# Low parts of weights and the S5 parameters moved from VectorE to GpSimd in a one-core model kernel

## The chip, the core and the metric

The kernel runs on one core of a Trainium2 chip. The metric is device time in microseconds (us), median of three runs. The engines are TensorE (PE in the rows, PEld for its weight loads), VectorE (DVE), ScalarE (ACT), GpSimd (POOL) and SyncE (SP), which issues the DMAs of the weight stream. They run side by side and meet at semaphores.

## The reference, cut to what matters

Two model blocks follow each other on 256 tokens of width 2048: four mixers (SSD, FOX attention, MLA attention, S5), each with a residual and a layer norm, then a mix of attention heads, a cross attention and a feed-forward part. All matmuls are float32. The part that is changed most is the S5 mixer:

```python
u, z = jnp.split(h @ w_in, 2, axis=-1)
lam = lax.complex(lam_re, lam_im)
step = jnp.exp(log_step)[:, None]
lam_bar = jnp.exp(lam * step)
b_bar = ((lam_bar - 1.0) / lam)[..., None] * lax.complex(b_re, b_im)
bu = jnp.einsum('gpi,btgi->btgp', b_bar, ug)
_, states = lax.associative_scan(_diag_linear_combine, (a_seq, bu), axis=1)
y = jnp.einsum('gip,btgp->btgi', c, states).real.reshape(bsz, T, S5_WIDTH) + d_skip * u
y = jax.nn.gelu(y)
y = y * jax.nn.sigmoid(y @ w_glu + b_glu)
y = y * jax.nn.silu(z)
```

## The kernel before, in words

**Weight slots.** All weights come as one stream of 575 slots of 128 x 2048 float32 (1 MB; some slots are narrower). A float32 product is made of three matmuls: high part by high part, low by high, high by low. For each slot SyncE loads `raw` (only two buffers: the load of slot n+2 is issued once the low part of slot n is made), ScalarE copies it rounded into the high part `WH` (`split_high`, L658), VectorE subtracts `raw - WH` into the low part `WL` (`split_low`, L666), and TensorE uses both (four buffers each). The splits run three slots (`LEAD`) ahead of TensorE. The semaphores `hi_ready`, `lo_ready` and `slots_used` count slots, so low parts have to be made in slot order.

**Order of the work.** Each engine has one program, written out by hand; nothing reorders it. What is in front in an engine's program has to be done first.

**End of a layer.** `last_out` (VectorE): for each half `tt` of the tokens it adds four output tiles to the residual `acc` with statistics (L766, L770), normalizes (`norm`: L908 and L913 for a layer norm), and for the first half the next layer's input is turned by TensorE (L821), copied by ScalarE into `XH` and made low by VectorE into `XL` (`turn_low`, L839). Three low parts of weights stand between these steps. GpSimd only computes the power -1/2 (L936), one for each half, in `norm_powers`. Four of the next stages (FOX, MLA, CROSS, FFN) start with `first_products`: TensorE multiplies the first token half with the slots X, X+1 and X+2 of the new stage, then turns groups 4 and 5 of the input (these need the second half's norm), then takes the second half. S5 does not: its `across` blocks wait for both halves.

**S5.** `s5_tensor` projects with `across` blocks (48 matmuls of one slot, L699 to L701) and runs 16 chunks of scan between them. VectorE first makes the parameters (powers of lambda, about 70 small instructions, L2362 to L2418) and then, for each chunk c:

- `scan(c)` (L2467 to L2486): waits for `v_done` (TensorE's L2120) and for the sine and cosine of the chunk, made by ScalarE from `turns5`, which GpSimd makes (L2606 to L2613); it also needs `ring5`, which GpSimd copies (L2617) after the scan before it
- `skip(c)` (L2492)
- the low part of slot n+7+2c
- `input_tables(c+1)` into `bs5` (L2432 to L2443); TensorE turns them (L2108), ScalarE copies them into `wb5` (L2226), and TensorE makes the next chunk's `v` from them (L2120)
- the low part of slot n+8+2c
- `output_tables(c+1)` into `cs5` (L2432 to L2441), for which TensorE waits at L2129 (`direct_of`)

Here n is `S5_SLOT`. `w5`, `bs5`, `cs5`, `small` (also called `q4`), `gain` and `offs` (which hold B and C of S5 here) lie in SBUF, `banks` in PSUM.

Of the kernel before, what the change touches and what calls it, by code (L numbers as in the profile page):

```python
# [24 lines left out]
P = 128  # L25
T = 256
# [301 lines left out]
def program(nc, a, keep):  # L328
# [17 lines left out]
    with ExitStack() as s:  # L346
        pows5 = sb("pows5", [P, 2, 5, 2, 64], within=s)
        x5 = sb("x5", [P, 2, 4, 64], within=s)
        ring5 = sb("ring5", [P, 4, 64], within=s)
    with ExitStack() as s:  # L350
        rvec = sb("rvec", [MIX_HEADS, N], within=s)
# [105 lines left out]
    with ExitStack() as s:  # L457
# [5 lines left out]
        dt5 = sb("dt5", [P, 4, P], within=s)  # L463
        w5 = sb("w5", [P, 4, T], within=s)
        trig5 = sb("trig5", [P, 2, T], within=s)
        turns5 = sb("turns5", [P, 2, T], within=s)
        jump5 = sb("jump5", [P, P], within=s)
        co5 = sb("co5", [P, 2, 64], within=s)
        d5 = sb("d5", [P, 64], within=s)
        bg5 = sb("bg5", [P, KC], within=s)  # L470
        halfpi = sb("halfpi", [P, 1], within=s)
        par5 = w5[:, :, :].rearrange("p a t -> p (a t)")[:, 0:192].rearrange("p (a t) -> p a t", a=3)
        tmp5 = w5[:, :, :].rearrange("p a t -> p (a t)")[:, 192:704].rearrange("p (a t) -> p a t", a=8)
# [105 lines left out]
    par_loaded = sem("par_loaded")  # L579
    s5_loaded = sem("s5_loaded")  # L580
    zeroed = sem("zeroed")
    co5_ready = sem("co5_ready")
# [77 lines left out]
    def split_low(dve, n, early=False):  # L660

        if n.it is None and (n.first >= SLOTS or (n.first in EARLY and not early)):
            return
        wait(dve, hi_ready, n, 1)
        at = slice(0, slot_width(n))
        nc.vector.tensor_tensor(WL[:, n.first % PARTS, at], raw[:, n.first % RAWS, at],  # L666
                                WH[:, n.first % PARTS, at].bitcast(F32), ALU.subtract).then_inc(lo_ready, 1)

# [188 lines left out]
    def last_out(dve, slot, i, norm, begun=False):  # L857
# [7 lines left out]
        split_low(dve, At(slot + 1 + LEAD))  # L865
# [3 lines left out]
        split_low(dve, At(slot + 2 + LEAD))  # L869
        if i is not None:  # L870
            turn_low(dve, i, 2, 4)
        split_low(dve, At(slot + 3 + LEAD))
# [3 lines left out]
        if i is not None:  # L876
            turn_low(dve, i, 4, 6)
# [61 lines left out]
    def norm_powers(pool):  # L939

        for tt in range(TT):
            served_pool[0] += 1
            power(pool, served_pool[0], tt, tt + 1)

# [933 lines left out]
    def mla_scalar(act):  # L1878
# [3 lines left out]
        nc.scalar.activation(cossin[:, 0, :, :], ang[:, :, :], ACT.Sin, scale=0.5).then_inc(act_done, 1)  # L1882
        for j in range(2):
# [49 lines left out]
        body(At(MLA_HEAD), At(MLA_SLOT + 9), At(0), True)  # L1933
        with act.Fori(1, 4) as it:
# [17 lines left out]
    def mla_vector(dve):  # L1952
# [12 lines left out]
        for s in range(8):  # L1965
            split_low(dve, At(MLA_SLOT + s + LEAD))
        dve.wait_ge(slots_used, MLA_SLOT + 9)
# [226 lines left out]
    def s5_scalar(act):  # L2194
        def reply():
            served_act[0] += 1
            act.wait_ge(act_asked, served_act[0])

# [64 lines left out]
        reply()  # L2263
        nc.scalar.activation(tmp5[:, TMP, :], par5[:, LSTEP, :], ACT.Exp).then_inc(act_done, 1)
        reply()
        nc.scalar.activation(tmp5[:, RADIUS, :], tmp5[:, RADIUS, :], ACT.Exp)
        nc.scalar.activation(tmp5[:, SIN1, :], tmp5[:, THETA, :], ACT.Sin)
        nc.scalar.activation(tmp5[:, SINH, :], tmp5[:, THETA, :], ACT.Sin, scale=0.5).then_inc(act_done, 1)
# [4 lines left out]
        act.wait_ge(zeroed, 1)  # L2273
# [84 lines left out]
    def s5_vector(dve):  # L2358
        n = S5_SLOT
        par, tmp = par5, tmp5  # L2360
        dve.wait_ge(par_loaded, 16)
        dve.drain().then_inc(act_asked, 1)  # L2362
        dve.wait_ge(xt_done, 32)
        scale_residual(dve)
        dve.wait_ge(act_done, ask("act"))
        nc.vector.tensor_tensor(tmp[:, RADIUS, :], par[:, LRE, :], tmp[:, TMP, :], ALU.mult)
        nc.vector.tensor_tensor(tmp[:, THETA, :], par[:, LIM, :], tmp[:, TMP, :], ALU.mult)
        dve.drain()
        whole_turns(dve, tmp[:, THETA, :], tmp[:, CRE, :])
        dve.drain().then_inc(act_asked, 1)  # L2370
        dve.wait_ge(zeroed, 1)
        nc.vector.tensor_scalar(co5[:, TURN4, :], tmp[:, THETA, :], 4 / TWO_PI, None, ALU.mult)
        for q in range(4):
            at = slice(32 * q, 32 * q + 32)
            nc.vector.tensor_copy(jump5[at, 32 * (3 - q):32 * (3 - q) + 32], ident[at, 32 * q:32 * q + 32])
        split_low(dve, At(n + 4))
        dve.wait_ge(act_done, ask("act"))

        nc.vector.tensor_tensor(tmp[:, SINH, :], tmp[:, SINH, :], tmp[:, SINH, :], ALU.mult)
        nc.vector.tensor_tensor(tmp[:, SIN1, :], tmp[:, SIN1, :], tmp[:, RADIUS, :], ALU.mult)  # L2380
        nc.vector.tensor_tensor(co5[:, R4, :], tmp[:, RADIUS, :], tmp[:, RADIUS, :], ALU.mult)
        dve.drain()
        nc.vector.scalar_tensor_tensor(tmp[:, SINH, :], tmp[:, SINH, :], -2.0, tmp[:, RADIUS, :], ALU.mult, ALU.mult)
        nc.vector.tensor_tensor(co5[:, R4, :], co5[:, R4, :], co5[:, R4, :], ALU.mult)
        dve.drain().then_inc(co5_ready, 1)
        nc.vector.scalar_tensor_tensor(tmp[:, SINH, :], tmp[:, RADIUS, :], -1.0, tmp[:, SINH, :], ALU.add, ALU.add)
        nc.vector.tensor_tensor(tmp[:, TMP, :], par[:, LRE, :], par[:, LRE, :], ALU.mult)
# [799 lines left out]
```

## Time and profile before

| | |
|---|---|
| median of 3 runs | 3800.28 us (3795.49 to 3802.94) |
| the profiled execution | 3803.58 us, its span 3801.9 us |
| busy: PE, DVE, ACT, POOL | 3463.6, 2466.8, 1563.2, 142.3 us |
| mean granted clock of TensorE | 0.958 of full speed |
| SSD ends, FOX starts | about 820 to 857 us |
| FOX ends, MLA starts | about 1327 to 1370 us |
| MLA ends, S5 starts | about 1818 to 1905 us |
| 16 chunks of the S5 scan | about 1905 to 2231 us |
| CROSS and FFN start | about 2940 and 3020 us |

The times of the rows below are microseconds from the span's start. A granted clock of 1.00 is 2.4 GHz and 0.50 is 1.2 GHz. The span is one execution, 3.3 us above the median of the runs.

### The profile page before, as it was taken

To read this page: it belongs to the slowest core of one execution; us is meant where nothing else is said; L and a number is where in the kernel's file an instruction comes from. 1 tells how busy PE (TensorE), PEld (TensorE's weight loads), DVE (VectorE), ACT (ScalarE), POOL (GpSimd) and SP (SyncE) were. 2 spreads that over 40 slices of the span, in tenths; PEclk is the share of its full clock that TensorE was granted. 3 is DMA by queue.
4 is the path that set the end of the run, shared out by engine and by line. 5 is a ranking of instruction groups with operands and counts; after the bars stand their busy time and mean duration, and the time that the engine had idled before them with its cause. 6 is when DMAs were issued, how large, how long until landed. Compare 5 with 4: busy or idle time off the path is not lost.

```text
span 3801.9 us, 48707 instructions
## 1 busy us (share of the span) xinstructions
PE 3463.6 (91%) x18186; PEld 2957.4 (78%) x18186; DVE 2466.8 (65%) x3189; ACT 1563.2 (41%) x1853; POOL 142.3 (4%) x176
## 2 busy tenths in 40 slices
PE   5899999979999978888699999888998799999998
PEld 5777778767888867776599988777887688888886
DVE  4677777775555664554799976856556665665655
ACT  3344444434444333333367654333333344334342
POOL 0000000000000000000122200100000000000000
PEclk8899999989999988999899999999999999999999
DMA  5455555534444443333223245575665355455553
GB/s 209 155 188 188 192 194 188 194 140 182 177 178 175 166 161 122 124 130 111 98 104 112 99 144 207 173 226 217 223 224 193 133 192 187 177 196 188 185 186 126
DMA packets 89264, 642.83 MB, mean 169 GB/s; under 512 B 10176, under 2 KB 10256, under 8 KB 11712
## 3 DMA queue, kind: packets, MB, share of 16 engines
q1 hardware_dynamic: 83376, 607.16, 44.4%
q0 software_dynamic: 5776, 34.13, 2.8%
q8 instruction: 76, 1.25, 0.1%
q14 instruction: 36, 0.29, 0.0%
HBM read 638.02 MB, written 3.23 MB: 169 GB/s over the span
## 4 chain that ended last, share of the span: by engine, by line
PE 59%; DVE 18%; issue 7%; DVEq 6%; ACT 5%; DMA 4%; ACTq 0%; POOL 0%; SPq 0%; POOLq 0%
PE banks L682 16%; PE banks L683 16%; PE banks L684 16%; DVE WL L666 6%; DMA raw<-in_stream 4%; ACT WH L658 3%; DVE xc L1264 1%; PE banks L1409 1%; DVEq L2444 1%; PE banks L699 1%; DVEq L2434 1%; PE banks L700 1%; PE banks L701 1%; DVEq L1212 1%; PE banks L990 1%
## 5 line engine op out<-in xcount | busy, mean ns | idle before, releaser
L666 DVE TENSOR_TENSOR WL<-raw,WH 128x2048 fp32r<-128x2048 f32 (+2 forms) x575 | 1249.0, 2175 | 694.1 <-ACT WH L658 685.5
L658 ACT ACTIVATE WH<-raw 128x2048 fp32r<-128x2048 f32 (+2 forms) x575 | 1045.6, 1821 | 1070.8 <-DMA raw<-in_stream 518.0
L682 PE MATMUL banks<-WH,XH 128*128 128x512 f32 (+2 forms) x2784 | 1070.0, 384 | 72.9 <-DVE WL L666 33.2
L684 PE MATMUL banks<-WH,XL 128*128 128x512 f32 (+2 forms) x2784 | 1044.8, 375 | 0.0
L683 PE MATMUL banks<-WL,XH 128*128 128x512 f32 (+2 forms) x2784 | 1044.5, 375 | 0.0
L682 PEld LDWEIGHTS banks<-WH,XH 128*128 128x128 f32 x2784 | 535.7, 192 | 172.3 <-issue 60.9
L684 PEld LDWEIGHTS banks<-WH,XL 128*128 128x128 f32 x2784 | 534.7, 192 | 82.2
L683 PEld LDWEIGHTS banks<-WL,XH 128*128 128x128 f32 x2784 | 536.1, 193 | 77.9 <-issue 0.5
L682 PE MATMUL banks<-WH,YH 128*128 128x512 f32 x976 | 395.9, 406 | 13.4 <-DVE acc L779 8.5
L683 PE MATMUL banks<-WL,YH 128*128 128x512 f32 x976 | 390.6, 400 | 0.0
L684 PE MATMUL banks<-WH,YL 128*128 128x512 f32 x976 | 387.7, 397 | 0.0
L682 PEld LDWEIGHTS banks<-WH,YH 128*128 128x128 f32 x976 | 185.8, 190 | 65.8 <-issue 16.5
L699 PE MATMUL banks<-XH,WH 128*128 128x256 f32 x768 | 224.1, 292 | 0.6 <-DVE XL L839 0.6
L684 PEld LDWEIGHTS banks<-WH,YL 128*128 128x128 f32 x976 | 185.4, 190 | 44.3
L683 PEld LDWEIGHTS banks<-WL,YH 128*128 128x128 f32 x976 | 185.6, 190 | 43.6 <-issue 1.7
L700 PE MATMUL banks<-XH,WL 128*128 128x256 f32 x768 | 218.9, 285 | 0.0
L701 PE MATMUL banks<-XL,WH 128*128 128x256 f32 x768 | 218.9, 285 | 0.0
L779 DVE TENSOR_TENSOR acc<-acc,banks 128x512 f32<-128x512 f32 x272 | 174.1, 681 | 27.6 <-PE banks L684 27.2
L699 PEld LDWEIGHTS banks<-XH,WH 128*128 128x128 f32 x768 | 149.4, 194 | 5.0 <-issue 3.9
L700 PEld LDWEIGHTS banks<-XH,WL 128*128 128x128 f32 x768 | 149.3, 194 | 0.1
L701 PEld LDWEIGHTS banks<-XL,WH 128*128 128x128 f32 x768 | 148.9, 194 | 0.0
L936 POOL TENSOR_TENSOR powout<-powin,con 128x1 f32<-128x1 f32 (+2 forms) x33 | 28.7, 870 | 2527.2 <-DVE powin L923 1187.8
(405 smaller groups left out, 3534.3 us busy)
## 6 DMA issues: line engine op xcount, KB each, us to landing
raw<-in_stream SPq DMA_DIRECT2D x575, 1024.0 KB, 4.8
gain<-in_gains POOLq DMA_DIRECT2D x9, 1024.0 KB, 5.1
arow<-acs_scratch POOLq DMA_DIRECT2D x8, 1024.0 KB, 5.0
offs<-in_ln_b POOLq DMA_DIRECT2D x4, 1024.0 KB, 7.3
acc<-in_x SPq DMA_DIRECT2D x2, 1024.0 KB, 6.6
src<-in_mem POOLq DMA_DIRECT2D x1, 2048.0 KB, 8.4
toep<-rvec_scratch POOLq DMA_DIRECT2D x4, 512.0 KB, 8.6
out_y<-src SPq DMA_DIRECT2D x2, 1024.0 KB, 3.9
```

The costliest lines, as they stand in the source:

```text
L658: nc.scalar.activation(WH[:, n.first % PARTS, at], raw[:, n.first % RAWS, at], ACT.Copy).then_inc(hi_ready, 1)
L666: nc.vector.tensor_tensor(WL[:, n.first % PARTS, at], raw[:, n.first % RAWS, at], WH[:, n.first % PARTS, at].bitcast(F32), ALU.subtract).t ...
L682: nc.tensor.matmul(out, xh[:, k0 + k, at], wh[:, k, lo:hi], start=start, stop=False)
L683: nc.tensor.matmul(out, xh[:, k0 + k, at], wl[:, k, lo:hi], start=False, stop=False)
L684: ins = nc.tensor.matmul(out, xl[:, k0 + k, at], wh[:, k, lo:hi], start=False, stop=stop)
L699: nc.tensor.matmul(out, wh[:, k, at], XH[:, 4 * s + k, :], start=start, stop=False)
L700: nc.tensor.matmul(out, wl[:, k, at], XH[:, 4 * s + k, :], start=False, stop=False)
L701: ins = nc.tensor.matmul(out, wh[:, k, at], XL[:, 4 * s + k, :], start=False, stop=stop)
L779: ins = nc.vector.tensor_tensor(at, at, pairs[pair][tt][:, :], ALU.add)
L990: ins = nc.tensor.matmul(bank[4 + c][:, e * 64:e * 64 + 64], em[:, c, e, :], xdt[:, c, e * 64:e * 64 + 64], start=True, stop=True)
L1212: dve.drain()
L1264: ins = nc.vector.scalar_tensor_tensor(xc[:, k, j:T], b[:, 0:T - j], cwg[:, 3 - j, k:k + 1], xc[:, k, j:T], ALU.mult, ALU.add)
```

## The change: what it does

1. **S5 scan.** The low part of slot n+8+2c, which stood between the two tables in VectorE's program, is made by GpSimd (`lows_beside`), in its iteration after the turns of the chunk and before the copy of `ring5`. It waits until all low parts before it are made.
2. **S5 parameters.** The powers are computed by GpSimd (`s5_powers`) during MLA, with two sines and two exponentials by ScalarE there too, and one reciprocal with its three inputs by VectorE. The turns of the first chunk, the clearing of buffers and the loads are in new places.
3. **Layer ends.** At the end of SSD, FOX, MLA, of the mix and of CROSS GpSimd makes the low parts of the slots X and X+1 of the next stage, between its two powers (`first_lows`). The low part of X+2 stays with VectorE and comes after the second half's norm.

```diff
+    def first_lows(pool, slot, r):
+        pool.wait_ge(src_ready, 4 * (r - 1) + 2)
+        lows_beside(pool, slot, slot + 2)
+
+    def lows_beside(pool, lo, hi):
+        for n in range(lo, hi):
+            pool.wait_ge(hi_ready, n + 1)
+            pool.wait_ge(lo_ready, n)
+            at = slice(0, slot_width(At(n)))
+            nc.gpsimd.tensor_tensor(WL[:, n % PARTS, at], raw[:, n % RAWS, at], WH[:, n % PARTS, at].bitcast(F32),
+                                    ALU.subtract).then_inc(lo_ready, 1)
@@ last_out, VectorE
         add_half(dve, slot, 1, 0)
-        split_low(dve, At(slot + 1 + LEAD))
         if i is not None:
             turn_low(dve, i, 0, 2)
         add_half(dve, slot, 1, 1)
-        split_low(dve, At(slot + 2 + LEAD))
         if i is not None:
             turn_low(dve, i, 2, 4)
-        split_low(dve, At(slot + 3 + LEAD))
         add_half(dve, slot, 1, 2)
         add_half(dve, slot, 1, 3)
         norm(dve, 1)
         if i is not None:
+            dve.wait_ge(lo_ready, slot + 3 + LEAD)
+            split_low(dve, At(slot + 3 + LEAD))
             turn_low(dve, i, 4, 6)
@@ norm_powers, GpSimd
+            if tt == 0 and slot is not None:
+                first_lows(pool, slot, r)
@@ mla_scalar
+        act.wait_ge(par_loaded, 16)
+        nc.scalar.activation(tmp5[:, TMP, :], par5[:, LSTEP, :], ACT.Exp).then_inc(step_ready, 1)
...
         body(At(MLA_HEAD), At(MLA_SLOT + 9), At(0), True)
+        act.wait_ge(theta_ready, 1)
+        nc.scalar.activation(tmp5[:, RADIUS, :], tmp5[:, RADIUS, :], ACT.Exp)
+        nc.scalar.activation(tmp5[:, SIN1, :], tmp5[:, THETA, :], ACT.Sin)
+        nc.scalar.activation(tmp5[:, SINH, :], tmp5[:, THETA, :], ACT.Sin, scale=0.5).then_inc(sines_ready, 1)
@@ mla_vector, before the copy of kpeT
+        nc.vector.tensor_tensor(tmp5[:, CRE, :], par5[:, LRE, :], par5[:, LRE, :], ALU.mult)
+        nc.vector.tensor_tensor(tmp5[:, CIM, :], par5[:, LIM, :], par5[:, LIM, :], ALU.mult)
+        dve.drain()
+        nc.vector.tensor_tensor(tmp5[:, CRE, :], tmp5[:, CRE, :], tmp5[:, CIM, :], ALU.add)
+        dve.drain()
+        nc.vector.reciprocal(tmp5[:, TMP2, :], tmp5[:, CRE, :]).then_inc(norm5_ready, 1)
@@ s5_vector (its parameters are taken out: L2362 to L2418)
         split_low(dve, At(n + 4))
+        dve.wait_ge(s5_loaded, 64)
+        dve.wait_ge(zeroed, 2)
+        dve.wait_ge(powers_ready, 1)
...
         input_tables(0)
         split_low(dve, At(n + 5))
         output_tables(0)
+        dve.wait_ge(xt_done, 32)
+        scale_residual(dve)
         split_low(dve, At(n + 6))
...
             scan(c)
             skip(c)
+            dve.wait_ge(lo_ready, n + 7 + 2 * c)
             split_low(dve, At(n + 7 + 2 * c))
             if c + 1 < CHUNKS5:
                 input_tables(c + 1)
-            split_low(dve, At(n + 8 + 2 * c))
             if c + 1 < CHUNKS5:
                 output_tables(c + 1)
@@ s5_pool
             pool.drain().then_inc(part_ready, 1)
             if c:
+                lows_beside(pool, S5_SLOT + 6 + 2 * c, S5_SLOT + 7 + 2 * c)
                 pool.wait_ge(scanned, c)
             nc.gpsimd.tensor_copy(ring5[:, :, 1:64], ...).then_inc(ring_ready, 1)
+        lows_beside(pool, S5_SLOT + 38, S5_SLOT + 39)
@@ GpSimd's program
-        norm_powers(pool)
+        norm_powers(pool, MLA_SLOT, 2)
...
+        pool.dma_start(par5, a["s5_par"]).then_inc(par_loaded, 16)
         power(pool, served_pool[0], 0, 4)
-        norm_powers(pool)
+        s5_powers(pool)
+        pool.wait_ge(headl_ready, MIX_HEAD)
...
+        norm_powers(pool, S5_SLOT, 3)
         s5_pool(pool)
```

VectorE's program in one chunk of the scan, from the low part of slot n+7+2c to the next chunk's first instruction, before:

```order
L666 TENSOR_TENSOR WL<-raw,WH 128x2048
L2432 TENSOR_TENSOR small<-gain,pows 128x256
L2433 TENSOR_TENSOR small<-gain,pows 128x256
L2439 TENSOR_TENSOR bs<-small 64x16x16 x2
L2432 TENSOR_TENSOR small<-gain,pows 128x256
L2433 TENSOR_TENSOR small<-gain,pows 128x256
L2443 TENSOR_TENSOR bs<-small 64x16x16 x2
L666 TENSOR_TENSOR WL<-raw,WH 128x2048
L2432 TENSOR_TENSOR small<-offs,pows 128x320
L2433 TENSOR_TENSOR small<-offs,pows 128x320
```

and now (L671 is the low part, L2400 to L2411 the tables):

```order
L671 TENSOR_TENSOR WL<-raw,WH 128x2048
L2400 TENSOR_TENSOR small<-gain,pows 128x256
L2401 TENSOR_TENSOR small<-gain,pows 128x256
L2407 TENSOR_TENSOR bs<-small 64x16x16 x2
L2400 TENSOR_TENSOR small<-gain,pows 128x256
L2401 TENSOR_TENSOR small<-gain,pows 128x256
L2411 TENSOR_TENSOR bs<-small 64x16x16 x2
L2400 TENSOR_TENSOR small<-offs,pows 128x320
L2401 TENSOR_TENSOR small<-offs,pows 128x320
```

The second low part is gone from between the tables. GpSimd's program for one chunk, before:

```order
L2606 TENSOR_TENSOR turns<-con,co 128x256
L2609 TENSOR_SCALAR turns<-turns 128x256
L2611 TENSOR_SCALAR turns<-turns 128x256
L2613 TENSOR_TENSOR turns<-turns 128x256
L2617 COPY ring<-co 128x4x63
```

and now (L685 is its low part):

```order
L2639 TENSOR_TENSOR turns<-con,co 128x256
L2642 TENSOR_SCALAR turns<-turns 128x256
L2644 TENSOR_SCALAR turns<-turns 128x256
L2646 TENSOR_TENSOR turns<-turns 128x256
L685 TENSOR_TENSOR WL<-raw,WH 128x2048
L2651 COPY ring<-co 128x4x63
```

It stands between the turns and the ring, and the ring waits behind it. VectorE's program at the end of SSD, from the second half's first addition to the FOX input's groups 4 and 5, before:

```order
L766 TENSOR_TENSOR acc<-acc,banks 128x512
L770 BN_STATS stats<-acc 128x6
L666 TENSOR_TENSOR WL<-raw,WH 128x2048
L839 TENSOR_TENSOR XL<-banks,XH 128x4x128 x2
L766 TENSOR_TENSOR acc<-acc,banks 128x512
L770 BN_STATS stats<-acc 128x6
L666 TENSOR_TENSOR WL<-raw,WH 128x2048
L839 TENSOR_TENSOR XL<-banks,XH 128x4x128 x2
L666 TENSOR_TENSOR WL<-raw,WH 128x2048
```

and now, from the second half's norm (L926, L931) on:

```order
L926 SCALAR_TENSOR_TENSOR acc<-acc,mv,gain 128x1024 x2
L931 SCALAR_TENSOR_TENSOR acc<-acc,powout,offs 128x1024 x2
L671 TENSOR_TENSOR WL<-raw,WH 128x2048
L858 TENSOR_TENSOR XL<-banks,XH 128x4x128 x2
L671 TENSOR_TENSOR WL<-raw,WH 128x2048
```

All three low parts are gone from ahead of the norm; the third (slot X+2) stands behind it and ahead of the input's groups 4 and 5.

## Rows read from the trace of the kernel before

**Rows 1.** Busy times of the whole span: engine, us, share, instructions.
```profile
PE 3463.6 (91%) x18186; PEld 2957.4 (78%) x18186; DVE 2466.8 (65%) x3189; ACT 1563.2 (41%) x1853; POOL 142.3 (4%) x176
```
**Rows 2.** Stretches: us; busy of PE, PEld, DVE, ACT, POOL; clock; DMA share; GB/s.
```profile
1925.40:1945.80 20.40, 18.94 (x161) 18.60 (x162) 19.00 (x32) 12.58 (x28) 5.98 (x5) 1.00 0.28 103
1945.80:1966.40 20.60, 20.50 (x160) 19.53 (x160) 19.26 (x32) 14.92 (x35) 4.45 (x5) 0.92 0.30 103
```
**Rows 3.** VectorE in time, chunk 0 to chunk 1: start, us, instruction, idle before.
```profile
1912.23 2.29 DVE L666 TENSOR_TENSOR WL<-raw,WH 128x2048 fp32r<-128x2048 f32 x1
...
1919.07 2.29 DVE L666 TENSOR_TENSOR WL<-raw,WH 128x2048 fp32r<-128x2048 f32 x1 [0.17 <-issue]
1921.28 0.48 DVE L2432 TENSOR_TENSOR small<-offs,pows 128x320 f32<-128x320 f32 x1
...
1925.49 0.69 DVE L2467 TENSOR_TENSOR w<-banks,trig 128x512 f32<-128x512 f32 x1 [0.23 <-PE banks L2120]
```
**Rows 4.** GpSimd's instructions by form, whole span: count, busy us, mean ns, idle before.
```profile
L2606 POOL TENSOR_TENSOR turns<-con,co 128x256 f32<-128x256 f32 x16 | 33.6, 2099 | 83.9 <-ACT trig L2209 60.8 <-DVEq L2385 23.1
L2613 POOL TENSOR_TENSOR turns<-turns 128x256 f32<-128x256 f32 x16 | 12.1, 756 | 2.4
L2617 POOL COPY ring<-co 128x252 f32<-128x252 f32 x16 | 6.3, 395 | 172.5 <-DVEq L2477 172.3 <-issue 0.2
L2598 POOL MEMSET halfpi<- 128x1 f32 x1 | 0.1, 125 | 0.0
```
**Rows 5.** GpSimd beside VectorE in time: once alone, then where they meet.
```profile
1879.90 0.61 POOL L2606 TENSOR_TENSOR turns<-con,co 128x256 f32<-128x256 f32 x1 [23.09 <-DVEq L2385]
1912.55 3.11 POOL L2606 TENSOR_TENSOR turns<-con,co 128x256 f32<-128x256 f32 x1 [3.48 <-ACT trig L2209]
1957.95 0.77 POOL L2613 TENSOR_TENSOR turns<-turns 128x256 f32<-128x256 f32 x1
1957.70 0.43 DVE L2432 TENSOR_TENSOR small<-gain,pows 128x256 f32<-128x256 f32 x1
1958.04 0.96 DVE L2433 TENSOR_TENSOR small<-gain,pows 128x256 f32<-128x256 f32 x1
```
**Rows 6.** TensorE in time, chunks 1 and 2: outputs, tables turned, v, direct.
```profile
1938.39 0.39 PE L2145 MATMUL banks<-uy,dt 128*128 128x64 f32 x2
1940.10 1.03 PE L2108 MATMUL banks<-con,bs 128*128 128x128 f32 x8
1942.39 1.92 PE L2120 MATMUL banks<-uy,wb 128*128 128x64 f32 x16
1945.77 3.45 PE L2129 MATMUL banks<-cs,bs 128*32 128x128 f32 x16 [1.46 <-DVEq L2459]
```
**Rows 7.** Start of S5 in time: VectorE's parameters and first tables, TensorE's first turn.
```profile
1868.26 2.37 DVE L844 TENSOR_SCALAR acc<-acc 128x2048 f32<-128x2048 f32 x2
1891.43 0.42 DVE L2432 TENSOR_TENSOR small<-gain,pows 128x256 f32<-128x256 f32 x1
1895.01 1.97 PE L2108 MATMUL banks<-con,bs 128*128 128x128 f32 x8 [16.73 <-DVEq L2452]
1905.10 0.69 DVE L2467 TENSOR_TENSOR w<-banks,trig 128x512 f32<-128x512 f32 x1 [1.40 <-PE banks L2120]
```
**Rows 8.** End of SSD and start of FOX in time: VectorE's and TensorE's steps.
```profile
835.82 2.29 DVE L666 TENSOR_TENSOR WL<-raw,WH 128x2048 fp32r<-128x2048 f32 x1 [0.98 <-ACT WH L658]
838.26 0.47 PE L682 MATMUL banks<-WH,XH 128*128 128x512 f32 x1 [1.48 <-DVE WL L666]
845.50 1.97 PE L821 MATMUL banks<-con,acc 128*128 128x128 f32 x8 [4.28 <-DVE acc L913]
848.03 0.79 PE L682 MATMUL banks<-WH,XH 128*128 128x512 f32 x1 [0.56 <-DVE XL L839]
```
**Rows 9.** Table load of ScalarE in MLA, reciprocal of VectorE in S5, in time.
```profile
1370.09 1.28 ACT L1881 ACT_TABLE_LOAD   x1
1881.85 0.55 DVE L2396 RECIPROCAL w<-w 128x64 f32<-128x64 f32 x1
```

## Prediction of the change's time, made before it ran

> **What bounds the kernel now.** I read the busy times first, then the stretches of the S5 scan, then VectorE, GpSimd and TensorE in time inside a chunk, and last the two places where TensorE stands still: the start of S5 and the ends of layers. Over the span TensorE is busy 91% and GpSimd 4% [rows 1], so room on GpSimd is plain; whether it can be used is decided locally. In the scan a chunk takes 20.4 and 20.6 us, with TensorE busy 18.9 and 20.5 of it and VectorE 19.0 and 19.3 [rows 2]. VectorE has next to no idle time: 0.17 before a low part, 0.23 before the next scan [rows 3]. So VectorE sets the chunk, and TensorE is only 1.5 us behind it: in chunk 2 it waited 1.46 us for VectorE's output tables, and then its 16 small matmuls took 3.45 us [rows 6] at a mean granted clock near half, where they take 1.9 in other chunks; that is why the stretch with this wait shows 0.92 and the other 1.00 [rows 2].
>
> Below, t is the moment a chunk's scan starts on VectorE (1905.10, 1925.49, ...). In chunk 0 the first low part starts at t+7.1, the second at t+14.0, the output tables at t+16.2, the next scan at t+20.4 [rows 3, 7].
>
> **Part 1, the scan.** Removed from VectorE: one low part per chunk, 1921.28 - 1919.07 = 2.21 us and the 0.17 of idle before it, 2.4 us [rows 3]. Added on GpSimd: the same subtraction over 128x2048. If the two engines were independent, the gain would be capped by TensorE at 1.5 us a chunk.
>
> They are not independent. GpSimd's L2606 takes 0.61 alone and 3.11 where it starts 0.3 us after a low part of VectorE: it waited for it [rows 3, 5]. In the other direction, L2433 takes as much as its twin L2432 when free, 0.43; beside GpSimd's L2613, which runs 1957.95 to 1958.72, it ends at 1959.00, that is 0.28 us after GpSimd is done, though it began at 1958.04 [rows 5]. 256 elements of VectorE at the pace of its low part (2.29 us for 2048) are 0.29 us: the whole of its work came after GpSimd's last moment. So a two-input subtraction or product of GpSimd stops a two-input instruction of VectorE fully. The Trainium skill, "SBUF — State Buffer", section "SBUF: two separate sides", says this as a rule: the port pair shared by the two is an exclusive lock for the whole instruction, against VectorE's instructions with two SBUF inputs too. By that rule, the trace agrees (0.28 us), moving this work frees nothing.
>
> What does GpSimd's low part meet? It may start when VectorE's low part before it is done, at t+9.4. VectorE is then in the input tables, whose operands `small`, `gain`, `pows` are all in SBUF. GpSimd gets in between two of them, and the rest of the tables waits for its whole length T. None of VectorE's work up to the next scan reads PSUM, so nothing fills the gap.
>
> T is not in the trace. The nearest rows are GpSimd's two-input instructions on 256 elements: 0.756 on average for L2613 and 0.61 for L2606 alone [rows 4, 5]. With 0.125 of fixed time (the memset of one element [rows 4]) they give 2.47 and 1.89 ns an element, so for 2048 elements 5.2 and 4.0 us. The upper end is 8 x 0.756 = 6.05 (all of it grows with size); the lower is 2.3: the one-input copy's pace, (0.395 - 0.125) / 252 = 1.07 ns, times 2048, plus 0.125 [rows 4]. I take T = 4.5, between the two nearest forms. "GPSIMD Engine Reference" of the Trainium skill, section "Performance versus the Vector engine", has 4497 ns for a two-input add of this size; no run here shows it yet, and by it the sum would stay the same.
>
> VectorE's chunk then is 20.5 - 2.4 + 4.4 = 22.5 us (0.1 of T falls into a gap of VectorE). The four instructions for the turns meet VectorE's tables as before; I cost this at nothing, as they only move from the input to the output tables.
>
> TensorE comes late too. The input tables used to be done at about t+13; now at 13 + 4.4 = t+17.4. TensorE has finished the outputs at t+13.3 (1938.78) and a quarter block at t+15, and stands still for 2.4 us. Then it turns the tables (1.03), does a quarter block (1.7) and makes v (1.92) [rows 6]: t+22.0 at full clock, just in time. But 1.46 us of waiting was enough for a half clock over the next 3.45 us [rows 6], and the turn after the wait of 16.73 us took 1.97 instead of 1.03 [rows 6, 7]. With about 3.3 us at half clock behind each wait, v is ready at 17.4 + 1.97 + 2.0 + 1.9 = t+23.3. The old order had the low part as a buffer here: VectorE worked for 2.2 us while TensorE and ScalarE turned the tables. So I take 23.3 a chunk, +2.8, and this in the 15 chunks that have such a low part between their tables: **+42 us**. The 16th GpSimd low part, behind the last chunk, meets an idle VectorE: 0.
>
> **Part 2, the S5 parameters.** TensorE stands still for 16.73 us until 1895.01, so it was done with its first four blocks at 1878.3 [rows 7]. VectorE's parameters fill 1870.6 to 1891.4. Now VectorE goes from the last input group to a low part and the input tables (3.6 us, 1891.43 to 1895.0). The MLA end before it is shorter too (part 3), so that TensorE starts S5 about 3.9 us earlier and is done at 1874.4, and the tables at about 1871.5: TensorE no longer waits. Its turn comes at 1874.4, 20.6 us earlier. Scan 0 came 10.1 us after it [rows 7]. Will VectorE be ready? From 1871.5 it has a low part (2.2), output tables (4.0), the residual (2.4), a low part (2.2) and small copies (0.9), with waits to about 1884.4: yes, by nothing to spare. **-20.5 us**, between -24 (if TensorE gains on the clock) and -12 (if ScalarE's stacking comes late, since its third high part waits for a load).
>
> The moved work costs in MLA. VectorE: three small products and a reciprocal (0.55 [rows 9]) with pauses, 1.3 us, right before the copy on which TensorE waits there. ScalarE: an exponential between two sines means a table load of 1.28 [rows 9] ahead of two high parts, about 1.5; two more later, mostly in ScalarE's idle time, 0.7. GpSimd's 55 small instructions stop VectorE for fractions of a microsecond under waits of TensorE. **+3.5 us** (0 to 7).
>
> **Part 3, the layer ends.** VectorE loses three low parts and a wait of 0.98 before the second norm [rows 8], 7.8 us, of which about 2 come back as waits for ScalarE's copies. The additions there read PSUM, and GpSimd's two low parts (2 x 4.5) end before the second norm. So the norm ends about 5.3 us earlier. But at FOX, MLA, CROSS and FFN TensorE needs slot X+2 for the first token half, at 838.26, before it turns groups 4 and 5, at 845.50 [rows 8]; this low part now comes after the norm. New times at FOX: norm done 841.3, low part 843.5, 12 matmuls of 3 us (5.5 at half clock, as behind 848.03 [rows 8]) to 846.5 or 849.1, the turn 1 us, `XL` 1.5: the second half starts at 849.1 or 851.7 instead of 848.03, but the half clock is then behind it. That is -1.5 to +1.5 each; I take +0.75 x 4 = **+3 us** (-6 to +8). Only S5, whose first block waits for both halves anyway, keeps its 3.9, counted above.
>
> **The sum.** 42 - 20.5 + 3.5 + 3 = +28 us. The profiled execution took 3803.6 (3801.9 in the span), so 3831.6; it lies 3.3 above the median, from which the forecast is 3800.3 + 28 = **3828 us**.
>
> **Rivals.** (A) The forecast: the lock and T near 4.5. Chance 0.52; its own range is 3808 to 3848.
>
> (B) The same lock, with T near 6 or a slower TensorE. For it: a fixed time below 0.125, or a half clock that lasts through the turn, the quarter block and v. With T = 6.05 a chunk takes 23.3 + 1.55 = 24.9, +4.35, and 15 chunks +65; sum +51, 3851. Clock losses of 1 us more a chunk lead to 3866. Or Part 2 gives only -12: 3837. Against it: between the known forms T is 4 to 5.2. Chance 0.25.
>
> (C) The other side: GpSimd's instruction is short or hardly stops VectorE. For it: T could be near 2.3; one-input instructions of GpSimd delayed VectorE little. Break-even is where the chunks cost no more than 14 us in all, 0.93 a chunk. With a chunk of 18.8 + T that has to stay below 21.4, T must be below 2.6 where TensorE's chain at half clock decides, and 3.4 where VectorE does. At T = 2.3 VectorE's chunk is 20.3 and the sum is -20.5 + 6.5 - 3 = -17: 3783. With no lock at all TensorE's 19.0 bounds, -22 more: 3764. Against it: the 0.28 us of rows 5, at several places alike. Chance 0.13.
>
> (D) The pieces cancel: T about 3 to 3.5 and full clock, within 0.2% (7.6 us, about what a measurement of this kernel can tell from no change). Chance 0.10.
>
> That the low part isn't made beside the tables is no rival: the program order fixes it.
>
> Slower by over 0.2%: A and B, 0.77, with nearly all of A's range above 3808. Same: D, with a little of A, 0.10. Faster: C, 0.13. The range that holds 8 in 10 reaches from 3786 (T near its lower bound) to 3864 (B with clock losses).
>
> **What would show it.** In the changed profile: GpSimd's 128x2048 instructions of 4 to 5.2 us; in each chunk one table instruction of VectorE (L2400 to L2411) longer by about that much, ending 0.28 us after GpSimd's; a chunk period near 23.3 and a wait of TensorE for `bs5` of 2 to 3 us followed by a granted clock of 0.5; scan 0 starting 20 us earlier relative to the MLA end; no 16.7 us wait; a wait for the low part of X+2 of about 6 us at FOX. I am wrong if VectorE's tables keep their 0.42 us beside GpSimd, if the period stays at 20.5 or less, or if scan 0 does not move.

## The result, and the profile after

The changed kernel takes 3822.64 us (median of 5 runs, 3817.18 to 3824.67), the kernel before 3800.28 us (5 runs, 3795.49 to 3805.11): a ratio of 1.0052, 95% interval 1.0039 to 1.0065. It is slower by 22 us; the forecast was 3828. The profiled execution took 3818.23 us (span 3816.2), 14.6 above the profiled one of before, so the traces show less than the medians: the pair explains 14 of the 22 us. The rest is spread between executions. Some stretches vary from kernel to kernel with the same code in them. The changed kernel and the ten experiments share the code of MLA from its latent norm to its last norm, which took 411.3 to 411.6 us in six of these profiles and 407.7 to 415.7 in the others. The mix, the same in all, took 536 to 544 us.

The busy times of the changed kernel, against [rows 1]:

```profile
PE 3466.4 (91%) x18186; PEld 2963.2 (78%) x18186; DVE 2453.0 (64%) x3113; ACT 1566.9 (41%) x1857; POOL 276.3 (7%) x257
```

The group of VectorE's low parts fell by more than that:

```profile
L671 DVE TENSOR_TENSOR WL<-raw,WH 128x2048 fp32r<-128x2048 f32 (+2 forms) x549 | 1190.0, 2170 | 690.7 <-ACT WH L663 684.4
```

It was 1249.0 us for 575 before, 59.0 more; 26 low parts are gone. Yet VectorE's busy time fell by only 13.8 us, although the parameters left it too: its other instructions became longer. GpSimd's low parts by form (count, then busy us and mean ns, idle before):

```profile
L685 POOL TENSOR_TENSOR WL<-raw,WH 128x2048 fp32r<-128x2048 f32 x26 | 120.4, 4631 | 241.7 <-ACT WH L663 225.6 <-DVE acc L931 10.2 <-DVE src L947 5.3
```

T, which the forecast took as 4.5, is 4.63 on average. It is 4.55 where nothing is in its way.

**Where the time went.** Differences of the same instruction's start in the two traces, after minus before:

| point | after - before, us | step |
|---|---|---|
| end of FOX's first stage (residual scaled) | -0.7 | end of SSD: -0.7 |
| the same in MLA | -1.7 | end of FOX: -1.0 |
| MLA's last norm, first token half | +0.6 | moved parameters and the rest of MLA: +2.2 |
| scan 0 (1905.10 to 1882.96) | -22.1 | start of S5: -22.7 |
| scan 15 (2215.82 to 2230.57) | +14.8 | 15 chunks: +36.9 |
| next norm (2397.55 to 2407.54) | +10.0 | behind the last chunk: -4.8 |
| start of FFN | +12.4 | mix and CROSS: +2.4 |
| end | +14.3 | FFN: +1.9 |

**The scan.** Its chunks take 24.0, 23.5, 22.2, 23.2, 22.3, 22.3, 22.4, 22.3, 22.3, 23.5, 22.1, 23.8, 23.3, 26.4 and 24.0 us (the fourteenth was long before too, 24.9). Two patterns occur. First chunk 1, VectorE in time, with its low part, the input tables and the next scan:

```profile
1913.87 2.29 DVE L671 TENSOR_TENSOR WL<-raw,WH 128x2048 fp32r<-128x2048 f32 x1
...
1916.90 5.29 DVE L2407 TENSOR_TENSOR bs<-small 64x256 f32<-64x256 f32 x2
...
1930.51 0.69 DVE L2435 TENSOR_TENSOR w<-banks,trig 128x512 f32<-128x512 f32 x1 [1.29 <-PE banks L2153]
```

GpSimd and TensorE in the same chunk:

```profile
1916.84 4.55 POOL L685 TENSOR_TENSOR WL<-raw,WH 128x2048 fp32r<-128x2048 f32 x1 [15.21 <-ACT WH L663]
```

```profile
1924.66 1.09 PE L2141 MATMUL banks<-con,bs 128*128 128x128 f32 x8 [2.95 <-DVEq L2420]
1928.05 2.42 PE L2153 MATMUL banks<-uy,wb 128*128 128x64 f32 x16
```

The pair L2407 takes 5.29 us instead of 0.85: it stands still while GpSimd works. TensorE waits 2.95 us for the input tables, v takes 2.42 us instead of the 1.92 of [rows 6], and VectorE then waits 1.29 us for v. This is the chunk that the forecast drew; the chunks 0, 9, 11, 12 and 14 are like it. Chunk 10 has the same order and takes 22.1 us: TensorE's clock did not fall in it (experiment 9). Now chunk 6 (t = 2020.53), first ScalarE, then GpSimd, then VectorE:

```profile
2028.18 3.07 ACT L2247 ACTIVATE uy<-banks 32x256 f32<-32x256 f32 x8
2031.16 1.90 ACT L663 ACTIVATE WH<-raw 128x2048 fp32r<-128x2048 f32 x1
```

```profile
2033.14 4.55 POOL L685 TENSOR_TENSOR WL<-raw,WH 128x2048 fp32r<-128x2048 f32 x1 [13.19 <-ACT WH L663]
```

```profile
2032.23 0.85 DVE L2411 TENSOR_TENSOR bs<-small 64x256 f32<-64x256 f32 x2
2035.40 2.63 DVE L2400 TENSOR_TENSOR small<-offs,pows 128x320 f32<-128x320 f32 x1 [2.32 <-PE banks L2178]
2037.96 0.68 DVE L2401 TENSOR_TENSOR small<-offs,pows 128x320 f32<-128x320 f32 x1
```

In the chunks 2 to 7 ScalarE copies eight pieces of `uy` (here 3.07 us) ahead of the high part of slot n+8+2c. GpSimd therefore starts here at t+12.6 (t+12.1 to t+13.4 in the six chunks) and not at t+9.4, after the input tables. VectorE would go on to the output tables, but these overwrite `cs5`, and it has to wait for TensorE's outputs (L2178) first: 2.32 us here, 0.76 to 2.32 in the six. Part of the lock falls into this wait; the rest makes L2400 2.63 us long. It ends at 2038.03, 0.34 after GpSimd; 320 elements at VectorE's pace are 0.36. That is what [rows 5] showed, and it holds in all 15 chunks: the instruction that meets GpSimd ends 0.28 us after it with 256 elements and 0.34 or 0.35 with 320.

TensorE's waits over the scan, 1882 to 2250 us (us in total, times, longest):

```profile
PE banks L2141 <- DVEq L2420: 26.9, 9, 5.4
PE banks L2162 <- DVEq L2427: 17.7, 8, 3.4
PE banks L2176 <- DVE dt L2460: 2.6, 1, 2.6
```

All of TensorE's waits in the scan come to 47.2 us; before, they came to 17.7.

**The start of S5.** VectorE's first tables and TensorE's first turn, against [rows 7]:

```profile
1867.88 0.43 DVE L2400 TENSOR_TENSOR small<-gain,pows 128x256 f32<-128x256 f32 x1
```

```profile
1872.79 1.03 PE L2141 MATMUL banks<-con,bs 128*128 128x128 f32 x8
1880.59 2.00 PE L2153 MATMUL banks<-uy,wb 128*128 128x64 f32 x16 [1.02 <-ACT wb L2255]
```

The wait of 16.73 us is gone.

**The start of FOX.** VectorE and TensorE, against [rows 8]:

```profile
840.97 2.29 DVE L671 TENSOR_TENSOR WL<-raw,WH 128x2048 fp32r<-128x2048 f32 x1
```

```profile
843.40 0.76 PE L701 MATMUL banks<-WH,XH 128*128 128x512 f32 x1 [5.46 <-DVE WL L671]
...
847.95 1.03 PE L840 MATMUL banks<-con,acc 128*128 128x128 f32 x8
849.96 0.50 PE L701 MATMUL banks<-WH,XH 128*128 128x512 f32 x1 [0.98 <-DVE XL L858]
```

The low part of X+2 now makes TensorE wait 5.46 us, and of the 12 matmuls behind it the first eight or nine run at the lower clock, until 847.1. The second half starts at 849.96, 1.9 us later than before, but its first 12 matmuls take 3.0 us instead of 5.5. The lower clock lasts 6.8 us here and 10.2 us before (843.5 to 853.7).

Before the second norm GpSimd's two low parts run from 825.42 to 834.79. VectorE's additions in this time, which read `banks` in PSUM:

```profile
829.03 0.68 DVE L785 TENSOR_TENSOR acc<-acc,banks 128x512 f32<-128x512 f32 x1
832.72 0.68 DVE L785 TENSOR_TENSOR acc<-acc,banks 128x512 f32<-128x512 f32 x1
```

They take 0.68 us, as in the kernel before (829.98, 0.68): here GpSimd's instruction doesn't hold them up.

### The profile page after: what moved, and what is told of

It is laid out like the page before. It is cut to its first block, busy times and chain, and to the rows that moved or that the text cites. A ratio compares the mean times of both kernels' runs of the same rounds, so it can differ in the third digit from the quotient of the medians.

```text
span 3816.2 us, 48773 instructions
## 1 busy us (share of the span) xinstructions
PE 3466.4 (91%) x18186; PEld 2963.2 (78%) x18186; DVE 2453.0 (64%) x3113; ACT 1566.9 (41%) x1857; POOL 276.3 (7%) x257
## 4 chain that ended last, share of the span: by engine, by line
PE 58%; issue 16%; DVE 15%; DVEq 5%; ACT 3%; DMA 2%; POOL 1%; ACTq 0%; POOLq 0%; SPq 0%
PE banks L701 15%; PE banks L703 15%; PE banks L702 15%; DVE WL L671 4%; ACT WH L663 2%; DMA raw<-in_stream 2%; DVE xc L1284 1%; PE banks L718 1%; PE banks L719 1%; PE banks L720 1%; DVEq L2412 1%; DVE small L2400 1%; PE banks L757 1%; PE banks L758 1%; PE banks L759 1%
## 5 line engine op out<-in xcount | busy, mean ns | idle before, releaser
L671 DVE TENSOR_TENSOR WL<-raw,WH 128x2048 fp32r<-128x2048 f32 (+2 forms) x549 | 1190.0, 2170 | 690.7 <-ACT WH L663 684.4
L798 DVE TENSOR_TENSOR acc<-acc,banks 128x512 f32<-128x512 f32 x272 | 174.1, 682 | 23.6 <-PE banks L703 23.2
```

Source lines behind the costliest of these rows:

```text
L798: ins = nc.vector.tensor_tensor(at, at, pairs[pair][tt][:, :], ALU.add)
```

## The experiments

The sums are of the 15 periods of the scan in the profiled execution (before 310.7, changed 347.6). The kernel before was run again beside them: 3801.2 us with experiments 1 to 4, 3802.9 with 5 to 8, 3799.8 with 9 and 10 (medians). The ratios are against it. "One run" is a single execution.

**1. Both low parts of the scan back to VectorE.**

```diff
-            dve.wait_ge(lo_ready, n + 7 + 2 * c)
...
+            split_low(dve, At(n + 8 + 2 * c))
             if c + 1 < CHUNKS5:
                 output_tables(c + 1)
@@ s5_pool
-                lows_beside(pool, S5_SLOT + 6 + 2 * c, S5_SLOT + 7 + 2 * c)
```

> The changed kernel with VectorE making both low parts of a chunk again; S5 parameters and layer ends stay with GpSimd. Theory (the two-input instruction of GpSimd locks VectorE out, and this is the whole loss of the scan): the 15 chunk periods return from a mean of 23.2 us to 20.4 to 20.6, the profile loses 36.9 us in the scan and gives back the 4.7 us that the change gains behind the last chunk: median about 3790 us, faster than before by 10. Rival (the loss is in the turns and the ring copy in their new place in time, or in TensorE's clock): periods stay at 22 or more and the median stays above 3812.

Measured: 3777.8 us (5 runs), ratio 0.9940 (0.9927 to 0.9954). The sum is 308.3; scan 0 stays at 1882.95. So Part 1 alone costs 45 us of the medians and 39.3 of the scan, and the other two parts together gain 23. The periods came as expected, the median 12 us lower. I had expected 4.7 us to be given back behind the last chunk; it was about 2, and of the 44.3 us between the two spans 6.8 lie in the mix and in CROSS, whose code is the same in both. TensorE's wait in this scan:

```profile
PE banks L2162 <- DVEq L2427: 21.3, 15, 2.1
```

Nearly every chunk has a wait of 1.4 to 1.5 us, and the granted clock was 0.99 from 1950 to 2150 us, against 0.97 before and 0.96 in the changed kernel.

**2. Layer ends back to VectorE; scan and parameters as changed.**

```diff
         add_half(dve, slot, 1, 0)
+        split_low(dve, At(slot + 1 + LEAD))
...
+        split_low(dve, At(slot + 2 + LEAD))
...
+        split_low(dve, At(slot + 3 + LEAD))
```

> The changed kernel with all low parts of the layer ends back at VectorE; scan and parameters as changed. Theory (the four ends of FOX, MLA, CROSS and FFN gain nothing since slot X+2 waits behind the norm, S5 keeps about 4 us): median within 0 to 5 us above the changed kernel, 3823 to 3828. Rival (GpSimd's low parts there gain what VectorE loses, 5 us at each of five ends): 3845 or more.

Measured: 3828.0 us (4 runs), ratio 1.0071 (1.0056 to 1.0087), 5.4 above the changed kernel; the two intervals overlap. From MLA's last norm to scan 0 it takes 63.8 us (before 80.7, changed 58.0): the parameters gave 16.9 of it, the layer end 5.8.

**3. GpSimd makes half of each low part** (1024 columns, VectorE the rest).

```diff
-                lows_beside(pool, S5_SLOT + 6 + 2 * c, S5_SLOT + 7 + 2 * c)
+                half_low(pool, nc.gpsimd, S5_SLOT + 6 + 2 * c, 0).then_inc(half_made, 1)
@@ s5_vector
+            half_low(dve, nc.vector, n + 8 + 2 * c, 1)
+            dve.wait_ge(half_made, c + 1)
```

> The changed kernel with the moved low part of each chunk split in columns: GpSimd makes the first 1024, VectorE the last 1024 between its tables. Theory (the lock lasts as long as GpSimd's instruction, which grows with its size): GpSimd's 128x1024 takes 2.3 to 2.4 us, the period is 20.6 to 21.8. Rival (a fixed cost of any GpSimd instruction in this place, such as late starts): the period stays at 22.2 or more. Rival (no lock): 19.6 or less.

Measured: 3795.45 us (one run), sum 324.3, or 21.6 a chunk. By form:

```profile
L694 POOL TENSOR_TENSOR WL<-raw,WH 128x1024 fp32r<-128x1024 f32 x16 | 41.8, 2614 | 225.2 <-ACT WH L664 225.2
```

In one chunk GpSimd and then VectorE:

```profile
2025.42 3.42 POOL L694 TENSOR_TENSOR WL<-raw,WH 128x1024 fp32r<-128x1024 f32 x1 [14.27 <-ACT WH L664]
```

```profile
2025.38 1.23 DVE L694 TENSOR_TENSOR WL<-raw,WH 128x1024 fp32r<-128x1024 f32 x1 [0.37 <-ACT WH L664]
2028.98 0.54 DVE L2409 TENSOR_TENSOR small<-offs,pows 128x320 f32<-128x320 f32 x1 [2.38 <-POOL WL L694]
```

Here VectorE was first, by 0.04 us, and GpSimd waited: 3.42 us, of which 2.2 come after VectorE's end. The two halves ran one after the other. With a GpSimd instruction of half the width, 23 of the 39 us came back. The edit also gives VectorE half of the low part and a wait for GpSimd's half, so the period isn't the price of the length alone.

**4. One SBUF input instead of two** (GpSimd multiplies `raw` by 0; the low parts of the 15 slots are left out of the result).

```diff
+                nc.gpsimd.tensor_scalar(WL[:, n % PARTS, :], raw[:, n % RAWS, :], 0.0, None, ALU.mult).then_inc(lo_ready, 1)
```

> The changed kernel, where GpSimd's instruction in the scan multiplies raw by zero instead of subtracting, so that it has one input of the same size; the low parts of 15 slots are left out by that. Theory (only two-input instructions of GpSimd keep VectorE's two-input instructions out): it takes 5 to 6 us on GpSimd, the table instructions beside it keep 0.4 to 0.9 us, the period is 19.0 to 20.5. Rival (any GpSimd instruction of this size holds the port pair): one table instruction grows by the whole length, the period is 23.5 or more.

Measured: 3795.85 us (one run), sum 324.8. One chunk, GpSimd and then VectorE:

```profile
1965.99 5.37 POOL L2652 TENSOR_SCALAR WL<-raw 128x2048 fp32r<-128x2048 f32 x1 [11.44 <-ACT WH L663]
```

```profile
1966.51 3.47 DVE L2400 TENSOR_TENSOR small<-offs,pows 128x320 f32<-128x320 f32 x1 [0.43 <-PE banks L2178]
```

Neither theory holds. VectorE was stopped, so two inputs on GpSimd aren't needed. But L2400 ended at 1969.98, 1.38 us before GpSimd's end at 1971.36. With 0.34 for its own work it went free 1.7 us before that end, after 3.65 us of the 5.37; in all 15 chunks the instruction of VectorE that met GpSimd's ended 1.38 to 1.46 us before it. The chunk cost 1.1 us more than in experiment 1, against 2.6 with the two-input form. Why it is let go early stays open.

**5. TensorE's last quarter block ahead of the turn.**

```diff
-            across(i + 1, (2,))
+            across(i + 1, (2, 3))
             if c + 1 < CHUNKS5:
                 turn_inputs(c + 1)
-            across(i + 1, (3,))
```

> The changed kernel with TensorE doing the last quarter of a block ahead of the turn of the tables and not behind it. Theory A (in chunks of 23.2 us and more TensorE's chain from the input tables to v decides, and its waits with the half clock behind them): the waits for the input tables, 26.9 us in all, fall to under 10, and the long chunks to about 22.5, sum of the 15 periods 335 to 342 instead of 347.6. Theory B (VectorE behind GpSimd's lock decides in all chunks): the sum stays at 345 to 350.

Measured: 3819.66 us (one run), sum 346.2. The gain of theory A did not come. TensorE's waits, 1885 to 2250 us:

```profile
PE banks L2153 <- ACT wb L2254: 18.7, 16, 1.2
PE banks L2141 <- DVEq L2419: 10.2, 5, 4.1
```

The wait for the input tables fell from 26.9 to 10.2 us, but now TensorE waits for ScalarE's copy of the turned tables into `wb5`, which the quarter block had covered. This run doesn't settle what bounds a chunk, though: only part of the chunks wait for the input tables, and the edit puts a quarter block behind the wait of the others. Experiments 9 and 10 part the two patterns.

**6. The best version: experiment 1, and the low part of X+2 ahead of the second norm** at the four ends whose next stage starts with `first_products`.

```diff
+        third = slot + 3 + LEAD
+        if i is not None and i != 3:
+            dve.wait_ge(lo_ready, third)
+            split_low(dve, At(third))
         add_half(dve, slot, 1, 2)
```

(the diff is against the changed kernel with experiment 1's edit; for the other ends the low part stays where it was)

> As e1_scan_back (both low parts of a chunk by VectorE), and at the ends of SSD, FOX, mix and CROSS VectorE makes the low part of slot X+2 ahead of the second norm instead of behind it; at the end of MLA it stays behind. Theory (TensorE's wait of 5.5 us for X+2 takes back what the earlier norm gives): the second token half starts 2 to 3 us earlier at each of the four ends, median 3767 to 3772. Rival (the norm on VectorE is the chain there, and 3.6 us more ahead of it cost as much): 3775 to 3780, as e1_scan_back.

Measured: 3765.5 us (3762.1 to 3768.53, 4 runs), ratio 0.9904 (0.9890 to 0.9919), 12 us under experiment 1 and a little below the 3767 to 3772 that I expected. TensorE's waits at the start of FOX, 810 to 865 us:

```profile
PE banks L840 <- DVE acc L936: 1.7, 1, 1.7
PE banks L701 <- DVE WL L671: 1.6, 1, 1.6
```

The 5.46 us are gone, and FOX's residual is scaled at 854.26 instead of 858.15. Of these 3.9 us, 1.9 stand already at SSD's last norm, ahead of the edit. From that norm on FOX's start is 2.0 us shorter, from FOX's last norm on MLA's start 1.0, and FFN 6.4; the stretch with CROSS's start differs by less than it varies with the same code. The two spans differ by 11.8 us.

**7. Only the parameters moved** (experiment 1, and the ends back as in experiment 2).

> Only the S5 parameters by GpSimd in MLA; all low parts by VectorE, as before. Theory (parts add): scan 0 is reached 17 us earlier after the end of MLA, the chunks keep 20.5 us, the median is 3781 to 3785. Rival (the gain of the parameters came only together with the shorter layer end, since ScalarE's stacking would bound): 3790 or more.

Measured: 3784.2 us (6 runs), ratio 0.9954 (0.9942 to 0.9966). From MLA's last norm to scan 0 it takes 62.9 us, 17.8 less than before. The median is 18.7 us under that of the kernel before beside it.

**8. Experiment 1, but GpSimd makes low parts only at MLA's end** (`first_lows` for S5; the other ends as before).

> As e1_scan_back, but GpSimd makes the two low parts at the end of MLA only; the other four ends are as in the kernel before. Theory: FOX and MLA lose 1 us each against e1_scan_back, FFN gains 2, CROSS 0 to 1: median 3776 to 3779. Rival (GpSimd's low parts help at every end): 3783 or more.

Measured: 3785.8 us (5 runs), ratio 0.9954 (0.9941 to 0.9967), 8 us above experiment 1, or 6 when each is taken against the kernel before beside it; the intervals of the two ratios overlap. It came above the range of the theory (3776 to 3779) and would fit the rival. But the two traces don't put this at the four ends: the stretches that hold them are longer here by -0.6 (FOX), +1.0 (MLA), +2.4 (CROSS) and -1.3 us (FFN), together 1.5. The rest of the 11.4 us between the spans lies in stretches whose code is the same in both, most of it behind the scan (3.5) and in the mix (4.6), so the rival isn't shown.

**9. ScalarE's high part ahead of its other copies**, so that GpSimd can start earlier.

```diff
+            split_high(act, At(n + 8 + 2 * c))
             b = c // 2
             if 2 <= c < 8:
...
                 keep_z(c // 2 - 4)
-            split_high(act, At(n + 8 + 2 * c))
```

> The changed kernel with one difference: in ScalarE's program the high part of slot n+8+2c stands ahead of the eight copies of uy (chunks 2 to 7) and of z (every second chunk from 8), so that GpSimd's low part can start earlier. In the changed kernel GpSimd starts at t+9.9 in chunks 0 and 1 (no such copies ahead; periods 24.0 and 23.5) and at t+12.1 or later in chunks 2 to 7 (periods 22.2 to 23.2). Theory A (the place of the lock decides: in the input tables it delays TensorE's turn, wb and v as well, in the output tables only these tables): chunks 2 to 7 now start GpSimd near t+9.9 and take 23.3 to 24 us each; sum of the 15 periods 353 to 358 instead of 347.6. Theory B (VectorE waits for GpSimd in these chunks, so an earlier start is an earlier end): their periods fall to 20.5 to 21.5, sum 337 to 343.

Measured: 3823.79 us (one run), sum 355.3; 11 of the 15 periods are 23.3 to 23.6. TensorE's waits, 1885 to 2240 us:

```profile
PE banks L2141 <- DVEq L2420: 48.1, 15, 5.5
```

VectorE's in the same stretch:

```profile
DVE w L2435 <- PE banks L2153: 16.8, 12, 2.3
```

Theory A held. With GpSimd starting near t+9.9 in most chunks, TensorE waits 3.2 us a chunk for the input tables, and then VectorE waits for v: TensorE's chain decides, not VectorE's work. An earlier start of the slow instruction made the scan 7.7 us longer; the time of this one execution is 1 us above the changed kernel's median. What the clock costs shows in two chunks that follow each other, 9 and 10 (us; busy of PE, PEld, DVE, ACT, POOL; clock; DMA share; GB/s):

```profile
2093.02:2116.58 23.56, 20.61 (x161) 20.14 (x161) 21.11 (x32) 12.32 (x27) 8.49 (x6) 0.93 0.26 90
2116.58:2139.07 22.49, 19.12 (x161) 18.58 (x161) 21.12 (x31) 13.21 (x28) 8.49 (x6) 1.00 0.27 95
```

Both have a wait of 2.95 us for the input tables. In the second the clock doesn't fall behind it, and the chunk takes 22.5 us. Only chunk 3 (22.7 us) is like it; all others have the lower clock.

**10. GpSimd's low part behind the input tables.**

```diff
+                pool.wait_ge(bs_ready, c + 1)
                 lows_beside(pool, S5_SLOT + 6 + 2 * c, S5_SLOT + 7 + 2 * c)
```

> The changed kernel with one difference: GpSimd's low part in each chunk of the scan waits until VectorE has made the input tables of that chunk (bs_ready). Theory A (place of the lock decides): GpSimd starts near t+12.7 in every chunk, the input tables take 0.42 us an instruction everywhere, all periods are 22.2 to 22.5 but the one that waits for a load; sum 336 to 341, time 7 to 11 us under the changed kernel, near 3813. Theory B (only the length of the lock counts, 4.6 us of which VectorE loses wherever it is): sum 347 within 2, time within 3 us of the changed kernel's.

Measured: 3816.43 us (5 runs), ratio 1.0048 (1.0034 to 1.0063), sum 344.2: periods of 22.5 to 23.2, one of 26.4, one of 21.5. TensorE's waits, 1885 to 2240 us:

```profile
PE banks L2162 <- DVEq L2427: 40.9, 15, 4.4
```

The direction is theory A's, the size about half of it: the sum fell by 3.4 us, where 7 to 11 were expected. The median is 6.2 us lower, but its interval overlaps the changed kernel's. GpSimd starts at t+12.7 to t+13.4, and its end sets the output tables. Between this and experiment 9, the same instruction of the same length costs the scan 11 us more or less by where it meets VectorE. In the best of the places tried it costs 2.4 us a chunk against experiment 1.

## Why the prediction was right, step by step

**The direction and the cause: right.** GpSimd's two-input instruction stops VectorE's two-input instructions for its whole length. The 0.28 us of [rows 5] carried over to 2048 columns (0.34 us at 320 elements). The rule of the Trainium skill, "SBUF — State Buffer", section "SBUF: two separate sides", agrees with these rows. It says that the other engine is blocked for the whole instruction and makes no exception for a one-input instruction of GpSimd; there it differs from the trace of experiment 4, which shows 3.65 of 5.37 us.

**T = 4.5: right**, 4.55 undisturbed and 4.63 on average. The interpolation from [rows 4, 5], with a fixed part and a part per element, gave 4.0 to 5.2. It also gives 2.1 to 2.7 for half the width, where experiment 3 shows 2.35 to 2.39 undisturbed.

**"GpSimd ... may start when VectorE's low part before it is done, at t+9.4": the step that failed in six chunks.** I looked at what GpSimd waits for on VectorE, and not at ScalarE's high part, which stands behind 3.07 us of copies in chunks 2 to 7. There the lock comes in the output tables, and partly in a wait that I had not seen either (`cs5` is free only after L2178). These chunks took 22.2 to 23.2 us and not 23.3. In the six together the scan grew by 11.5 us where the forecast has 16.8, in the other nine by 25.4 against 25.2. In the trace of before the wait did not show: the low part stood there and covered it.

**TensorE's chain at half clock (5.9 us from the input tables to the next scan): right where it applies.** In experiment 9, which puts the chunks into the order of the forecast, the common period is 23.5 to 23.6; I had 23.3. TensorE's wait is 2.95 us in most chunks against 2.4. The forecast's other value, 22.5 for VectorE alone, is the period of the chunks in which the clock stayed up (22.5 and 22.7). One premise was too strong: that 1.46 us of waiting is enough for the lower clock. In the kernel before the lower clock came behind each of six such waits; in experiment 1 it came at most twice behind thirteen waits of 1.2 to 1.8 us.

**The sum of Part 1:** forecast +42, the traces show +36.9 over the 15 chunks. The stretch behind the last one is 4.8 us shorter; I had no term for it, and it isn't shown to come from the change, since the same code took 182.0 us in experiment 5 (181.7 before, 177.0 changed). Against experiment 1, that is with all else equal, it is 39.3 in the scan and 45 in the medians.

**Part 2: right.** Forecast -20.5 for S5's start, with 3.9 of it from the layer end; measured -22.7, with 16.9 to 17.8 from the parameters (experiments 2 and 7) and 5 to 6 from the layer end. The cost in MLA, forecast +3.5, is +2.3: from the scaled residual to the latent norm, where ScalarE's first exponential and VectorE's reciprocal now stand, MLA takes 42.3 us before, 44.6 changed, 44.5 to 44.8 in nine of the ten experiments and 46.1 in experiment 5. The rest of MLA, with GpSimd's small instructions in it, took 411.4 and 411.3.

**Part 3: right within its bounds, a little dear.** Forecast +3 for the four ends, -6 to +8. The traces of before and after give -0.7, -1.0, +0.9 and +1.9, together +1.1; those of experiments 8 and 1 give -1.5, with the effect on the medians (-8, or -6 against the kernel before beside each) larger than the traces place, which stays open. Counted from the norm of the first token half on, all profiles agree on three ends: with the changed ends FOX's start is 0.3 to 0.9 us and MLA's 1.4 to 1.5 us shorter, and FFN 0.4 to 2.0 us longer; at CROSS the spread hides it. The mechanism at FOX was as told (norm at 841.0, low part behind it, a wait of 5.5 us, the lower clock over most of the 12 matmuls of X+2). Its price was smaller because the new wait stands for two old ones (1.48 and 4.28 us, [rows 8]): the half clock comes once either way, for 6.8 us now and 10.2 before. Experiment 6 shows that the wait for X+2 was real; without it the kernel is 12 us faster, 6.4 of them in FFN.

**The sum:** +28 forecast, +14.6 in the profiled pair, +22 in the medians. Against the traces the terms are off by -5.1 (scan), -4.8 (behind the scan, no term), -2.2 (S5's start), -1.3 (MLA), -1.9 (layer ends) and +1.5 (the mix, no term): nearly all of one sign. That the medians agree with the forecast to 6 us is therefore partly luck of the executions.

## What to carry to other kernels

By these traces, work moved from VectorE to GpSimd isn't parallel when both read two SBUF operands: price it at GpSimd's length on VectorE's time, and look for a place where VectorE reads PSUM or stands idle; here that was before the scan (parameters under MLA) and at the layer ends (additions from PSUM), and those two parts alone gave 0.6%, with one low part put back in its place 1.0%. For a moved instruction list all engines that release it, ScalarE's order too, and ask what wait the removed instruction had been covering. A change made of parts should be run in parts: this one hid a gain of 23 us behind a loss of 45.

## What the runs showed of the hardware

- A one-input instruction of GpSimd on 128 x 2048 float32 was no faster than the two-input one: 5.37 to 5.48 us against 4.55 to 4.63. It held back VectorE for its first 3.65 us only, in all 15 chunks. Why is open.
- The lock has no preference: 0.04 us of head start of VectorE made GpSimd's 2.2 us instruction last 3.42 (experiment 3).
- The granted clock doesn't follow the sum of TensorE's waits. From 1950 to 2150 us it was 1.00 in experiment 7 and 0.99 in experiment 1, with a wait of 1.4 to 1.5 us in nearly every chunk, and 0.97 in the kernel before, where waits of the same length came only in every second chunk. It was 0.96 in the changed kernel and 0.91 in experiment 2, with 47.2 and 46.1 us of waits in the scan. What makes the difference no run here shows.
